# Seven block products for eight in one unit of each strip pair of the output product of an encoder block

## Chip, cores and metric

The kernel runs on one core of a Trainium2 chip. The metric is the time of one execution on the device in microseconds. The median of three timed runs of the kernel before is 1622.01 us (1621.78 to 1622.18).

## What is computed

One layer of an encoder over 256 tokens of width 2048, in float32: a combined input projection, a Mamba-2 branch in both directions, an attention branch, their gated sum, an output product with a residual, an MLP of width 8192, and a last norm. The change lies in the output product and its residual:

```
merged = sigmoid(gate_a) * branch_a + sigmoid(gate_b) * branch_b
x = x + merged @ w_out[layer]                 # (256 x 2048) @ (2048 x 2048)
h2 = rms_norm(x, g_mlp[layer])
x = x + jnp.square(jax.nn.relu(h2 @ w_mlp_in[layer])) @ w_mlp_out[layer]
return rms_norm(x, g_final)
```

## The kernel before

**Precision.** Every float32 operand of a product is split in two parts. ScalarE writes the high part (L637, `whi`), VectorE subtracts it from the raw piece for the low part (L1022, `wlo`), and TensorE makes three passes: high by high, high by low, low by high (`three_passes`, L1719 to L1721).

**Windows and pieces.** The work is a list of windows written out by hand in `walk`; every engine walks the same list. A window is a product of the 256 tokens with one strip of 512 columns of a weight matrix, in eight pieces of two row tiles each (512 KB, one load). For a piece TensorE issues 2 row tiles x 2 token blocks x 3 passes = 12 matmuls 512 columns wide. The output product is four windows, `out` 0 to 3; behind them stands the first window of the MLP.

**Positions.** Each engine runs, at each piece position, the splits that are due there and then the side work of the window, given as a list of names: `merged` (gates the product of the window before, adds the branches, turns the result and splits it), `residual` (adds a strip of the output product to `x_sb`, turns it by eight transposes, splits it and squares it). An engine's program order is fixed: what stands behind a waiting instruction waits too. PSUM is eight banks of 512 columns, the four of `G` and the four of `S`.

**Rings.** Up to the MLP the split weights have a ring of four slots: the copy on ScalarE of piece m waits until TensorE is done with piece m-4, and VectorE subtracts piece m at position m-2 of its own list. From the MLP on (`N_MLP`), the ring has eight slots (`whi_late`, `wlo_late`), and `count_due` lets both engines go up to seven blocks ahead. The raw pieces have four slots before the MLP and seven in it; SyncE issues the load of a piece once the low part of the piece that held its slot is made.

**Merged and output product.** The last window of the attention up-projection, (16, 1), fills `G[0:2]`. At position 0 of window (17, 0) VectorE makes the splits due there and then `gated`, which drains `G[0:2]` and raises `taken[1]`, and `merge_v`; TensorE turns the result behind piece 1. `out` 0 writes `G[2:4]` in all its eight pieces, `out` 1 writes `G[0:2]`. The last load of `x`, by SyncE, stands ahead of the load of piece 8 of the output product and waits for `merge_v` 4.

**Seven for eight.** In the MLP's second product the kernel already works with pairs of strips. A unit there is four row tiles by two strips, cut in 2 x 2 blocks of the tokens and of the weights. In a crossed unit VectorE makes four sums of weight blocks in place in the four raw slots (`difference`, L1025), four sums of the activations' blocks, and TensorE makes seven block products of 6 matmuls (`seven`) in place of four pieces of 12. Their results land in four banks, are copied out by ScalarE (L967) and added into `x_sb` in five additions by VectorE (L1515 to L1530).

Of the kernel before, what the change touches and what calls it, by code (L numbers as in the profile page):

```python
# [66 lines left out]
def walk(eng, window):  # L67
# [49 lines left out]
TURNED = 2  # L117
N_MLP = U_MLP * PIECES
# [11 lines left out]
MIX_OUT = {0: 4, 1: 5}  # L130
PAIR_PARTS = ((0, 0), (0, 1), (1, 1), (1, 0))
# [14 lines left out]

def crossed(n):

    at = pair_place(n)
    return at is not None and at[2] in CROSSED[at[1]]  # L150


def crossed_before(g, q, unit):

    return g * (len(CROSSED[0]) + len(CROSSED[1])) + q * len(CROSSED[0]) + CROSSED[q].index(unit)
# [6 lines left out]
def count_blocks():  # L162

    begin, at = [], 0
    for n in range(N_END):
        begin.append(at)
        if not crossed(n):
            at += 1
        elif pair_place(n)[3] == 3:
            at += len(PAIR_BLOCKS)  # L170
    return begin + [at]
# [5 lines left out]
def block_slot(m):  # L177
    return m % RING if m < N_MLP else (m - N_MLP) % LATE_RING

# [6 lines left out]
def released(n):  # L186

    if not crossed(n):
        return BLOCK[n] + 1
    part = pair_place(n)[3]  # L190
    return BLOCK[n] + (4, 5, 6, 7)[part]
# [12 lines left out]
def block_sources():  # L204

    out = []
    for n in range(N_END):
        if not crossed(n):
            out.append((n, None))
        elif pair_place(n)[3] == 3:  # L210
            out += [(n - 3, i) for i in range(len(PAIR_BLOCKS))]
    return out
# [20 lines left out]
def slot_free(m):  # L233

    if m < N_MLP + RING:
        return max(m - RING + 1, 0)
    return max(m - LATE_RING + 1, N_MLP)
# [24 lines left out]
def build(nc, x, x_t, w_in, w_dt, gains_in, taps_in, rows_in, w_ssm_up, w_attn_up, w_out, w_mlp_in, w_mlp_out,  # L262
# [208 lines left out]
    h_taken, c_taken = sem("h_taken"), sem("c_taken")  # L471
    mix_a, mix_v, x_mixed = sem("mix_a"), sem("mix_v"), sem("x_mixed")
# [46 lines left out]
    def out_product(j, tb):  # L519

        return S[:, 2 + tb, :] if j == 3 else product(j % 2, tb)
# [29 lines left out]
    def _(sp):  # L551
# [19 lines left out]
        def window(r, par, kind, idx, sides):  # L571
            for p in range(PIECES):
# [10 lines left out]
                if kind == "out" and (idx, p) in ((0, 0), (1, 0)):  # L583

                    sp.wait_ge(merge_v, 3 + idx)
                    for c in range(3 * idx, 3 + idx):
                        sp.dma_start(x_sb[:, c, :, :], x_k[:, :, c * N:(c + 1) * N]).then_inc(s_x[c], 16)
# [12 lines left out]
                elif kind == "mlp_pair":  # L600
                    g, q, unit, part = pair_place(n)
                    kh, half = PAIR_PARTS[part]
                    src = mats["mlp_out"][:, ds(g * KT + 4 * unit + 2 * kh, 2), (2 * q + half) * N:(2 * q + half + 1) * N]
                elif kind == "mlp_out":
# [27 lines left out]
    def _(act):  # L632
# [6 lines left out]
        def split(m):  # L639
# [5 lines left out]
            g, q, unit, _ = pair_place(n)  # L645
            turn = 4 * crossed_before(g, q, unit)
# [9 lines left out]
        def split_high(rnd, dst, k0, gain=None, factor=1.0):  # L656

            act.wait_ge(ts_t, rnd + 1)
# [5 lines left out]
            else:  # L664
                for c in range(4):
                    last = act.activation(dst[:, k0 + c, :], S[:, c // 2, c % 2 * T:(c % 2 + 1) * T],
# [250 lines left out]
        def residual(p, j, pr, pp):  # L917
            if p == 2:
                split_high(TS_X2 + j, a_hi, 4 * j, gain=1)
# [3 lines left out]
            if p == 7 and j == 3:  # L923
# [21 lines left out]

        def wide(t, h):
            return t[:, 2 * h:2 * h + 2, :].rearrange("p b n -> p (b n)")
# [25 lines left out]
        def finish(p, j, pr, pp):  # L973
            if p == (6 if j == 2 else 1 + j):
                act.wait_ge(c_taken, 14 + 2 * j)
                for tb in range(TB):
# [3 lines left out]
                                         residual, hidden, finish)}  # L980
        between_splits = {f.__name__: f for f in (carry_out, mix_out)}
# [37 lines left out]
    def _(dve):  # L1019
# [7 lines left out]
        def split(m):  # L1027
# [4 lines left out]
            g, q, unit, _ = pair_place(n)  # L1032
            turn = 4 * crossed_before(g, q, unit)
# [20 lines left out]
        def split_low(rnd, hi, lo, k0, gain=None, factor=1.0):  # L1054

            dve.wait_ge(ts_hi, rnd + 1)
# [6 lines left out]
            else:  # L1063
                for c in range(4):
                    k = gain * KT + k0 + c
                    last = dve.scalar_tensor_tensor(
                        out=lo[:, k0 + c, :], in0=S[:, c // 2, c % 2 * T:(c % 2 + 1) * T],
# [378 lines left out]
        def add_product(j, pr, pp, bank):  # L1446
            dve.wait_ge(used, done(pr, pp))
            dve.wait_ge(s_x[j], 16)
            for tb in range(TB):
                part = x_sb[:, j, tb, :]  # L1450
                last = dve.tensor_tensor(part, part, bank(tb), ALU.add)
            last.then_inc(taken[pp], 1)

        def residual(p, j, pr, pp):
            if p == 0:
                add_product(j, pr, pp, lambda tb: out_product(j, tb))
            if p == 2:
                split_low(TS_X2 + j, a_hi, a_lo, 4 * j, gain=1)
            if p == 4 and j == 3:
# [5 lines left out]
        def hidden(p, idx, pr, pp):  # L1465
# [15 lines left out]
            if p == 3 and j in SUMMED:  # L1481
                a11, a12 = hidden_u[:, 0:2, 0:P], hidden_u[:, 2:4, 0:P]
                a21, a22 = hidden_u[:, 0:2, P:T], hidden_u[:, 2:4, P:T]
                turn = 4 * (len(SUMMED) * g + j)
                dve.tensor_tensor(s_sum[:, 0, :, :], a21, a22, ALU.add).then_inc(s_v, 1)
                dve.tensor_tensor(s_sum[:, 2, :, :], a11, a21, ALU.subtract).then_inc(s_v, 1)
                dve.wait_ge(s_v, turn + 1)
                dve.tensor_tensor(s_sum[:, 1, :, :], s_sum[:, 0, :, :], a11, ALU.subtract).then_inc(s_v, 1)
                dve.wait_ge(s_v, turn + 3)
                dve.tensor_tensor(s_sum[:, 3, :, :], a12, s_sum[:, 1, :, :], ALU.subtract).then_inc(s_v, 1)  # L1490
# [65 lines left out]
        def finish(p, j, pr, pp):  # L1556
# [10 lines left out]
            if p == late + 2:  # L1567
                dve.wait_ge(c_taken, 14 + 2 * j)
                dve.wait_ge(s_g_last, 16)
                for tb in range(TB):  # L1570
# [3 lines left out]
                                         residual, hidden, sums, mixed, mix_out, finish)}  # L1574

        def window(r, par, kind, idx, sides):
            for p in range(PIECES):
                for m in due(piece_number(r, par, p), LEAD_LO):
                    split(m)
# [37 lines left out]
    def _(pool):  # L1617
# [73 lines left out]
        def residual(p, j, pr, pp):  # L1691
            if p == 4 and j == 3:
# [3 lines left out]
        table = {f.__name__: f for f in (rates, scan, zgate, rope, attend, residual)}  # L1696
# [16 lines left out]
    def _(pe):  # L1713
        operand = {"ssm_up": (b_hi, b_lo), "out": (b_hi, b_lo), "mlp_out": (b_hi, b_lo)}
# [21 lines left out]
        def transpose_round(src):  # L1736

            for c in range(4):
                for tb in range(TB):
                    last = pe.transpose(S[:, c // 2, c % 2 * T + tb * P:c % 2 * T + (tb + 1) * P],  # L1740
# [177 lines left out]
        def residual(p, j, pr, pp):  # L1918
            if p == 1:
                pe.wait_ge(taken[pp], pr + 1)  # L1920
                split_round(TS_X2 + j, lambda c, tb: x_sb[:, j, tb, c * P:(c + 1) * P])
            if p == 6 and j == 3:

                pe.wait_ge(rstd_x, 2)
# [5 lines left out]
        table = {f.__name__: f for f in (rates, decays, conv, scan, zgate, rope, attend, merged, residual)}  # L1930
# [13 lines left out]
        def seven(block, q, unit, m, start, stop):  # L1944
# [4 lines left out]
                    "b21": sums_bank(q, 0, 0), "b22": sums_bank(q, 1, 0), "t4": sums_bank(q, 0, 1)}  # L1949
            if block in ("b11", "t2", "t3", "t1"):  # L1950
                first_one, last_one = start, stop
            else:
                first_one, last_one = False, (block, q, unit) == ("b22", 1, 2)
# [3 lines left out]
            else:  # L1957
                i, tb = ("t1", "t2", "t3", "b22").index(block), 0
                hi, lo = s_hi[unit][:, i, :, :], s_lo[unit][:, i, :, :]
# [43 lines left out]

        def turned_window(r, idx, sides):
# [28 lines left out]
        def window(r, par, kind, idx, sides):  # L2033
            hi, lo = operand.get(kind, (a_hi, a_lo))
            if kind == "mlp_pair":
                pair_window(r, par, idx)
                return
            if kind == "xbc" and idx >= TURNED:
# [4 lines left out]
            elif kind == "mlp_in" and idx[0]:  # L2043
                if idx[1]:
                    pe.wait_ge(c_taken, 4 * idx[0])
                else:
                    pe.wait_ge(m_out, 4 * idx[0] - 1)
            elif kind == "mlp_out":
# [9 lines left out]
            rounds = {"ssm_up": TS_MERGED, "out": TS_X2, "mlp_in": TS_END}.get(kind)  # L2058
            ready = ts_lo
            late = (kind == "out" and idx == 0) or (kind == "mlp_in" and first(idx[0]) and idx[1] == 0)  # L2060
            into = product
            if kind == "out":
                into = lambda _, tb: out_product(idx, tb)
# [5 lines left out]
            for p in range(PIECES):  # L2069
                if (r, par) == (0, 0):  # L2070
                    pe.wait_ge(x_lo, 2 * p + 2)
                if p == 0 and rounds is not None:
                    pe.wait_ge(ready, rounds - 1 if late else rounds)
                if p == 0 and kind == "mlp_in" and idx[1] == 1:
                    pe.wait_ge(hid_hi, 1)
                if p == PIECES - 2 and late:
                    pe.wait_ge(ready, rounds)
# [95 lines left out]
```

## Time and profile before

| | |
|---|---|
| median of three runs | 1622.01 us |
| profiled execution, own time | 1622.15 us |
| its span, first to last instruction | 1620.0 us |
| output product, four windows (838.72 to 929.35 us of the span) | 90.63 us |
| TensorE (PE) busy in them | 90.63 us |
| VectorE (DVE) busy in them | 50.86 us |
| ScalarE (ACT) busy in them | 42.60 us |

The profile is of one execution. Times inside it run from the start of the span. Busy times of PE are of pipelined matmuls, which overlap each other; on VectorE and ScalarE too the end of one instruction overlaps the start of the next by a little.

### The profile page before, as it was taken

Reading aid. Unit: us, or ns where it says so; the run is one execution under the profiler, and the core shown is the slowest. Engines: PE = TensorE matmul, PEld = TensorE weight load, DVE = VectorE, ACT = ScalarE, POOL = GpSimd, SP = SyncE. Lnnn points to the kernel's source line nnn. Section 1 sums busy time; section 2 is a strip of 40 time slices with the busy share of each in tenths; the row PEclk is TensorE's granted clock in tenths of the full one; section 3 lists DMA queues with packets and bytes.
Section 4 is the critical chain, followed back from the end, with each engine's and each line's share of the span. In section 5 each row is a group of like instructions: output and inputs, shape, how many; then the busy total and the mean of one; then the engine's idle time right before and its main releaser. Section 6 shows DMA issues by size and latency. Waiting matters only on the chain.

```text
span 1620.0 us, 20751 instructions
## 1 busy us (share of the span) xinstructions
PE 1608.5 (99%) x8104; PEld 1362.2 (84%) x8104; DVE 1264.1 (78%) x1520; ACT 917.1 (57%) x1262; POOL 79.1 (5%) x67
## 2 busy tenths in 40 slices
PE   9999999999999999999999999999999999999998
PEld 7888888888888888888888888888888888888886
DVE  7888878888666677776665576999799988998893
ACT  6666556666565445544444555665556556655562
POOL 3000000000001134000000000000000000000000
PEclk9999999999999999999999999999999999999999
DMA  7666665666556664445576676458646764586471
GB/s 272 202 200 190 189 200 189 208 195 203 183 186 182 191 187 153 142 145 175 187 229 195 225 236 187 144 182 285 184 125 224 262 190 134 194 282 209 148 245 53
DMA packets 134194, 312.21 MB, mean 193 GB/s; under 512 B 9744, under 2 KB 10448, under 8 KB 133968
## 3 DMA queue, kind: packets, MB, share of 16 engines
q1 hardware_dynamic: 129376, 302.21, 58.4%
q10 hardware_dynamic: 4720, 8.68, 2.0%
q8 instruction: 64, 1.05, 0.3%
q14 instruction: 34, 0.28, 0.0%
HBM read 308.68 MB, written 2.16 MB: 192 GB/s over the span
## 4 chain that ended last, share of the span: by engine, by line
PE 96%; DVE 2%; issue 1%; ACT 0%; POOL 0%; DMA 0%; POOLq 0%; DVEq 0%
PE G L1719 17%; PE G L1720 17%; PE G L1721 17%; PE G L1728 13%; PE S L1728 7%; PE G L1732 6%; PE S L1719 4%; PE S L1721 4%; PE S L1720 4%; PE S L1732 4%; PE S L1740 1%; PE S L1847 1%; DVE wlo L1022 1%; PE S L1891 0%; PE S L1824 0%
## 5 line engine op out<-in xcount | busy, mean ns | idle before, releaser
L637 ACT ACTIVATE whi<-raw 128x1024 fp32r<-128x1024 f32 x395 | 417.0, 1059 | 418.1 <-PE G L1721 254.9
L1022 DVE TENSOR_TENSOR wlo<-raw,whi 128x1024 fp32r<-128x1024 f32 x395 | 482.5, 1236 | 128.7 <-ACT whi L637 127.4
L1719 PE MATMUL G<-whi,a_both 128*128 128x512 f32 x768 | 301.3, 392 | 2.3 <-DVE wlo L1022 1.7
L1721 PE MATMUL G<-whi,a_both 128*128 128x512 f32 x768 | 299.5, 390 | 0.0
L1720 PE MATMUL G<-wlo,a_both 128*128 128x512 f32 x768 | 299.5, 390 | 0.0
L1728 PE MATMUL G<-a_both,whi 128*128 128x512 f32 x640 | 201.7, 397 | 0.0
L1719 PEld LDWEIGHTS G<-whi,a_both 128*128 128x128 f32 x768 | 144.3, 188 | 33.3 <-issue 2.6
L1721 PEld LDWEIGHTS G<-whi,a_both 128*128 128x128 f32 x768 | 144.2, 188 | 30.1
L1720 PEld LDWEIGHTS G<-wlo,a_both 128*128 128x128 f32 x768 | 144.3, 188 | 28.7
L1732 PEld LDWEIGHTS G<-a_both,wlo 128*128 128x128 f32 x640 | 120.3, 188 | 28.2
L1719 PE MATMUL G<-whi,b_hi 128*128 128x512 f32 x342 | 133.9, 392 | 0.0
L1720 PE MATMUL G<-wlo,b_hi 128*128 128x512 f32 x342 | 133.6, 391 | 0.0
L1721 PE MATMUL G<-whi,b_lo 128*128 128x512 f32 x342 | 133.3, 390 | 0.0
L637 ACT ACTIVATE whi_late<-raw 128x1024 fp32r<-128x1024 f32 x85 | 88.9, 1058 | 67.2 <-PE S L1732 22.0
L1732 PE MATMUL G<-a_both,wlo 128*128 128x256 f32 x640 | 125.9, 278 | 0.0
L1022 DVE TENSOR_TENSOR wlo_late<-raw,whi_late 128x1024 fp32r<-128x1024 f32 x85 | 102.6, 1221 | 24.7 <-ACT whi_late L637 24.1
L637 ACT ACTIVATE whi_late<-gates 128x1024 fp32r<-128x1024 f32 x67 | 70.0, 1056 | 49.7 <-PE G L1732 17.9
L1728 PEld LDWEIGHTS G<-a_both,whi 128*128 128x128 f32 x640 | 97.6, 189 | 0.1
L1022 DVE TENSOR_TENSOR wlo_late<-gates,whi_late 128x1024 fp32r<-128x1024 f32 x67 | 81.1, 1221 | 18.7 <-ACT whi_late L637 18.6
L637 ACT ACTIVATE whi<-gates 128x1024 fp32r<-128x1024 f32 x63 | 66.2, 1056 | 38.2 <-PE G L1732 13.9
L1022 DVE TENSOR_TENSOR wlo<-gates,whi 128x1024 fp32r<-128x1024 f32 x63 | 76.3, 1222 | 12.5 <-ACT whi L637 12.0
L1728 PE MATMUL G<-a_both,whi_late 128*128 128x512 f32 x256 | 80.5, 396 | 0.0
(306 smaller groups left out, 2692.4 us busy)
## 6 DMA issues: line engine op xcount, KB each, us to landing
raw<-in_w_in SPq DMA_DIRECT2D x208, 512.0 KB, 4.3
raw<-in_w_mlp_in SPq DMA_DIRECT2D x74, 512.0 KB, 4.0
raw<-in_w_mlp_out SPq DMA_DIRECT2D x74, 512.0 KB, 5.0
gates<-in_w_mlp_in SPq DMA_DIRECT2D x54, 512.0 KB, 4.0
gates<-in_w_mlp_out SPq DMA_DIRECT2D x54, 512.0 KB, 4.9
raw<-in_w_ssm_up SPq DMA_DIRECT2D x32, 512.0 KB, 3.8
raw<-in_w_attn_up SPq DMA_DIRECT2D x32, 512.0 KB, 4.6
raw<-in_w_out SPq DMA_DIRECT2D x32, 512.0 KB, 4.6
```

The costliest lines, as they stand in the source:

```text
L637: act.activation(high(m), piece(n), ACT.Copy).then_inc(hi_made, 1)
L1022: dve.tensor_tensor(low(m), piece(n), high(m).bitcast(F32), ALU.subtract).then_inc(lo_made, 1)
L1719: pe.matmul(out_ap, hi[:, k, cols], w_hi, start=start, stop=False)
L1720: pe.matmul(out_ap, hi[:, k, cols], w_lo, start=False, stop=False)
L1721: return pe.matmul(out_ap, lo[:, k, cols], w_hi, start=False, stop=stop)
L1728: pe.matmul(banks[:, c, :], high(m)[:, cols[kk]], a_both[:, 2 * p + kk, :, :].rearrange("p h t -> p (h t)"), start=(p + kk == 0), stop=False)
L1732: last = pe.matmul(banks[:, c, 0:T], low(m)[:, cols[kk]], a_hi[:, 2 * p + kk, :], start=False, stop=(2 * p + kk == KT - 1))
L1740: last = pe.transpose(S[:, c // 2, c % 2 * T + tb * P:c % 2 * T + (tb + 1) * P], src(c, tb), ident[:, :])
L1847: last = pe.matmul(S[:, 2, (4 * c + h) * HD:(4 * c + h + 1) * HD], mw[:, 0, h, c, :], tm[:, c, h * HD:(h + 1) * HD], start=True, stop=True)
```

## The change

The four windows of the output product become two pairs of strips: window (17, 0) and (17, 1) are pair 0, (18, 0) and (18, 1) pair 1. Sixteen pieces of a pair go by units of four row tiles, each unit with the order (rows 0, strip 0), (rows 0, strip 1), (rows 1, strip 1), (rows 1, strip 0). Unit 2 (pieces 8 to 11 of the pair) is made of seven block products. The direct products of pair 0 go to `G` and its mixes to `S`; pair 1 the other way round. The ring of eight split slots and its schedule start with the output product (`N_OUT`), while the raw ring keeps its four slots up to the MLP.

```
-    window(16, 1, "attn_up", 3, [("merged", 2)])
-    window(17, 0, "out", 0, [("merged", 3)])
-    window(17, 1, "out", 1, [("residual", 0)])
-    window(18, 0, "out", 2, [("residual", 1)])
-    window(18, 1, "out", 3, [("residual", 2)])
-    window(19, 0, "mlp_in", (0, 0), [("residual", 3)])
+    window(16, 1, "attn_up", 3, [("merged", 2), ("blend", 0)])
+    window(17, 0, "out_pair", (0, 0), [("merged", 3)])
+    window(17, 1, "out_pair", (0, 1), [("out_mix", 0)])
+    window(18, 0, "out_pair", (1, 0), [("out_sums", 0)])
+    window(18, 1, "out_pair", (1, 1), [("out_mix", 1)])
+    window(19, 0, "mlp_in", (0, 0), [("out_sums", 1)])
...
+OUT_CROSSED = 2
+OUT_MIX = 4
...
-    return m % RING if m < N_MLP else (m - N_MLP) % LATE_RING
+    return m % RING if m < N_OUT else (m - N_OUT) % LATE_RING
...
-        if m < N_MLP + LEAD_HI:
+        if m < N_OUT + LEAD_HI:
             when.append(m - lead)
         else:
-            when.append(max(STEP[m - MLP_LEAD], STEP[m] - LEAD_HI - (m - N_MLP) // RING, N_MLP))
+            when.append(max(STEP[m - MLP_LEAD], STEP[m] - LEAD_HI - (m - N_OUT) // RING, N_OUT))
```

VectorE's new side work: `blend` makes the four sums of the activations of unit 2, `out_mix` adds the copied banks in two additions of 512 columns (position 5), two of 1024 (position 6) and one of 1024 (position 7), `out_sums` adds the direct products and splits the turned strips. `out_sums` stands ahead of the splits of its position.

```
+        def blend(p, _, pr, pp):
+            if p == 4:
...
+                dve.tensor_tensor(hidden_u, b_hi[:, k, :].bitcast(F32), b_lo[:, k, :].bitcast(F32), ALU.add
+                                  ).then_inc(o_v, 1)
+                dve.wait_ge(o_v, 1)
+                blocks_summed(o_v, 1)
+            if p == 5:
+                dve.wait_ge(o_hi, 1)
+                dve.tensor_tensor(s_lo[OUT_SET][:, :, :, :], s_sum, s_hi[OUT_SET][:, :, :, :].bitcast(F32), ALU.subtract
+                                  ).then_inc(o_lo, 1)
...
+        def out_mix(p, q, pr, pp):
+            m, own = m_acc[q], x_sb[:, 2 * q:2 * q + 2, :, :]
+            if p == OUT_MIX + 1:
...
+            if p == OUT_MIX + 2:
...
+            if p == OUT_MIX + 3:
...
+        def out_sums(p, q, pr, pp):
+            if p < 2:
+                j = 2 * q + p
+                dve.wait_ge(used, done(pr, pp))
+                dve.wait_ge(o_mixed, q + 1)
+                for tb in range(TB):
+                    part = x_sb[:, j, tb, :]
+                    dve.tensor_tensor(part, part, out_bank(q, p, tb), ALU.add).then_inc(o_taken, 1)
+            if p in (2, 3):
+                j = 2 * q + p - 2
+                split_low(TS_X2 + j, a_hi, a_lo, 4 * j, gain=1, banks=out_turned(q, p - 2))
```

ScalarE copies the four mix banks in two instructions at position 4 of the windows (17, 1) and (18, 1), ahead of the splits due there. TensorE:

```
+        def out_sums(p, q, pr, pp):
+            if p in (1, 2):
+                j = 2 * q + p - 1
+                pe.wait_ge(o_taken, 2 * j + 2)
+                transpose_round(lambda c, tb: x_sb[:, j, tb, c * P:(c + 1) * P], out_turned(q, p - 1)
+                                ).then_inc(ts_t, 1)
...
+        def out_window(r, par, idx, sides):
+            for p in range(PIECES):
+                n = piece_number(r, par, p)
+                q, unit, part = out_place(n)
+                if (unit, part) == (0, 0):
+                    if q:
+                        pe.wait_ge(o_mix, 2)
+                    else:
+                        pe.wait_ge(taken[0], r)
+                        pe.wait_ge(ts_lo, TS_X2 - 1)
+                if (q, unit, part) == (0, 0, 1):
+                    pe.wait_ge(taken[1], r)
+                if (unit, part) == (OUT_CROSSED, 0):
+                    pe.wait_ge(o_lo, 1)
+                    pe.wait_ge(ts_lo, TS_X2 + 2 * q)
...
```

## Rows read from the trace of the kernel before

**Rows 1.** The page: span, busy time of the engines.

```profile
span 1620.0 us, 20751 instructions
...
PE 1608.5 (99%) x8104; PEld 1362.2 (84%) x8104; DVE 1264.1 (78%) x1520; ACT 917.1 (57%) x1262; POOL 79.1 (5%) x67
```

**Rows 2.** TensorE's waits for other engines, two longest of four: us, times, longest.

```profile
PE G L1719 <- DVE wlo L1022: 1.7, 2, 1.3
PE S L1752 <- DVE tmp_a L1074: 1.5, 1, 1.5
```

**Rows 3.** Busy time by stretch: the output product's four windows.

```profile
core 0: us, PE busy (x) PEld busy (x) DVE busy (x) ACT busy (x) POOL busy (x), PEclk, DMA share, GB/s
838.72:929.35 90.63, 90.63 (x417) 75.41 (x417) 50.86 (x55) 42.60 (x58) 0.00 (x0) 1.00 0.64 205
```

**Rows 4.** Groups by shape, 832 to 950 us: splits and strip additions.

```profile
L1022 DVE TENSOR_TENSOR wlo<-raw,whi 128x1024 fp32r<-128x1024 f32 x39 | 47.4, 1223 | 33.3 <-ACT whi L637 33.3
L637 ACT ACTIVATE whi<-raw 128x1024 fp32r<-128x1024 f32 x39 | 41.2, 1061 | 54.6 <-PE G L1721 40.8 <-PE S L1721 11.6 <-DMA raw<-in_w_out 2.3
L1719 PE MATMUL G<-whi,b_hi 128*128 128x512 f32 x96 | 37.7, 392 | 0.0
```

**Rows 5.** Timeline of TensorE, start of `out` 0: its 1st and 13th matmul, the transposes.

```profile
838.56 0.39 PE L1719 MATMUL G<-whi,b_hi 128*128 128x512 f32 x1
...
841.28 0.39 PE L1719 MATMUL G<-whi,b_hi 128*128 128x512 f32 x1
...
844.00 1.03 PE L1740 MATMUL S<-ident,tmp_b 128*128 128x128 f32 x8
```

**Rows 6.** Timeline of VectorE at the start of `out` 0.

```profile
838.76 1.28 DVE L1423 SCALAR_TENSOR_TENSOR gates<-gates,G 128x512 f32<-128x512 f32 x2 [0.34 <-PE G L1721]
840.08 1.23 DVE L1441 TENSOR_TENSOR tmp_b<-gates 128x1024 f32<-128x1024 f32 x1
```

**Rows 7.** ScalarE and VectorE at 929 us, where the eight-slot ring starts now.

```profile
929.43 1.06 ACT L637 ACTIVATE whi<-raw 128x1024 fp32r<-128x1024 f32 x1 [1.66 <-PE S L1721]
...
930.52 1.23 DVE L1022 TENSOR_TENSOR wlo<-raw,whi 128x1024 fp32r<-128x1024 f32 x1 [1.49 <-ACT whi L637]
931.66 1.22 DVE L1022 TENSOR_TENSOR wlo_late<-gates,whi_late 128x1024 fp32r<-128x1024 f32 x1
932.80 1.28 DVE L1451 TENSOR_TENSOR gates<-gates,S 128x512 f32<-128x512 f32 x2
```

**Rows 8.** VectorE in the MLP: a crossed unit's pace, then a pair's mixes.

```profile
1083.76 1.22 DVE L1022 TENSOR_TENSOR wlo<-gates,whi 128x1024 fp32r<-128x1024 f32 x1
1084.90 1.22 DVE L1025 TENSOR_TENSOR gates<-gates 128x1024 f32<-128x1024 f32 x1
...
1114.00 0.69 DVE L1515 TENSOR_TENSOR mt<-mt 128x512 f32<-128x512 f32 x1
...
1115.34 1.22 DVE L1022 TENSOR_TENSOR wlo<-gates,whi 128x1024 fp32r<-128x1024 f32 x1
...
1119.13 1.22 DVE L1524 TENSOR_TENSOR gates<-gates,mt 128x1024 f32<-128x1024 f32 x1
1120.38 1.23 DVE L1526 TENSOR_TENSOR mt<-mt 128x1024 f32<-128x1024 f32 x1
```

**Rows 9.** ScalarE in the MLP: the copies of four mix banks.

```profile
1052.46 1.92 ACT L967 ACTIVATE mt<-S 128x1024 f32<-128x1024 f32 x2
```

**Rows 10.** Loads: landing of 28 from 833.6 us, then 8 in a burst (1043 to 1051).

```profile
L610 SPq DMA_DIRECT2D raw<-in_w_out x28: 367/368/368, 833.6 to 909.2; - x28
...
DMA to landing us min/median/max: 3.8/4.5/5.9
...
DMA to landing us min/median/max: 4.3/6.8/7.3
```

**Rows 11.** Stretches at the ends of the span: TensorE's gaps, and its clock.

```profile
20.00:25.00 5.00, 3.69 (x17) 2.76 (x16) 3.34 (x2) 5.00 (x7) 4.84 (x3) 1.00 0.91 322
...
1610.00:1620.00 10.00, 2.40 (x11) 1.67 (x9) 2.69 (x7) 2.03 (x6) 0.94 (x1) 0.79 0.28 106
```

More of the change, by code:

```diff
@@ L582, in window @@
                     rope_parameters()
-                if kind == "out" and (idx, p) in ((0, 0), (1, 0)):
-                    sp.wait_ge(merge_v, 3 + idx)
-                    for c in range(3 * idx, 3 + idx):
+                if kind == "out_pair" and (idx[0], p) == (0, 0):
+                    half = idx[1]
+                    sp.wait_ge(merge_v, 3 + half)
+                    for c in range(3 * half, 3 + half):
                         sp.dma_start(x_sb[:, c, :, :], x_k[:, :, c * N:(c + 1) * N]).then_inc(s_x[c], 16)
@@ L654, in split, with split_high @@
             high_part(m, n)
-        def split_high(rnd, dst, k0, gain=None, factor=1.0):
+        def split_high(rnd, dst, k0, gain=None, factor=1.0, banks=(S, 0)):
+            bank, b0 = banks
             act.wait_ge(ts_t, rnd + 1)
@@ L1052, in split, with split_low @@
                 low_part(m, n + i - 3)
-        def split_low(rnd, hi, lo, k0, gain=None, factor=1.0):
+        def split_low(rnd, hi, lo, k0, gain=None, factor=1.0, banks=(S, 0)):
+            bank, b0 = banks
             dve.wait_ge(ts_hi, rnd + 1)
@@ L1444, in merged, with blocks_summed @@
                 split_low(j + TS_MERGED, b_hi, b_lo, j * 4, factor=0.5)
[L1446 to L1459, printed above, removed]
+        def blocks_summed(signal, before):
+            a11, a12 = hidden_u[:, 0:2, 0:P], hidden_u[:, 2:4, 0:P]
+            a21, a22 = hidden_u[:, 0:2, P:T], hidden_u[:, 2:4, P:T]
+            dve.tensor_tensor(s_sum[:, 0, :, :], a21, a22, ALU.add).then_inc(signal, 1)
+            dve.tensor_tensor(s_sum[:, 2, :, :], a11, a21, ALU.subtract).then_inc(signal, 1)
+            dve.wait_ge(signal, before + 1)
+            dve.tensor_tensor(s_sum[:, 1, :, :], s_sum[:, 0, :, :], a11, ALU.subtract).then_inc(signal, 1)
+            dve.wait_ge(signal, before + 3)
+            dve.tensor_tensor(s_sum[:, 3, :, :], a12, s_sum[:, 1, :, :], ALU.subtract).then_inc(signal, 1)
@@ L1942, in last_window, with seven @@
                 last.then_inc(fin_mm, 1)
-        def seven(block, q, unit, m, start, stop):
+        def seven(block, q, unit, m, start, stop, sums=sums_bank, set_of=None):
             a11, a12 = (slice(4 * unit + 2 * i, 4 * unit + 2 * i + 2) for i in range(2))
@@ L1952, in seven @@
             else:
-                first_one, last_one = False, (block, q, unit) == ("b22", 1, 2)
+                first_one, last_one = False, set_of is None and (block, q, unit) == ("b22", 1, 2)
             if block in left:
@@ L2002, in pair_window @@
                     last.then_inc(used, 1)
+        def out_window(r, par, idx, sides):
+            for p in range(PIECES):
+                n = piece_number(r, par, p)
+                q, unit, part = out_place(n)
+                if (unit, part) == (0, 0):
[9 more added lines that the diff above has]
+                    pe.wait_ge(ts_lo, TS_X2 + 2 * q)
+                m = BLOCK[n]
+                if unit == OUT_CROSSED:
+                    for i in range(2 * part, min(2 * part + 2, len(PAIR_BLOCKS))):
+                        pe.wait_ge(lo_made, m + i + 1)
+                        seven(PAIR_BLOCKS[i], q, unit, m + i, True, True, out_bank, OUT_SET).then_inc(used, 1)
+                else:
+                    kh, half = PAIR_PARTS[part]
+                    pe.wait_ge(lo_made, m + 1)
+                    for kk in range(2):
+                        k, cols = 4 * unit + 2 * kh + kk, slice(kk * N, (kk + 1) * N)
+                        for tb in range(TB):
+                            last = three_passes(out_bank(q, half, tb), k, tb, b_hi, b_lo, high(m)[:, cols],
+                                                low(m)[:, cols], k == 0, k == KT - 1)
+                    last.then_inc(used, 1)
+                for name, at in sides:
+                    if name in table:
+                        table[name](p, at, *previous(r, par))
         def turned_window(r, idx, sides):
@@ L2056, in window @@
                 pe.wait_ge(taken[par], r)
-            rounds = {"ssm_up": TS_MERGED, "out": TS_X2, "mlp_in": TS_END}.get(kind)
+            rounds = {"ssm_up": TS_MERGED, "mlp_in": TS_END}.get(kind)
             ready = ts_lo
-            late = (kind == "out" and idx == 0) or (kind == "mlp_in" and first(idx[0]) and idx[1] == 0)
+            late = kind == "mlp_in" and first(idx[0]) and idx[1] == 0
             into = product
-            if kind == "out":
-                into = lambda _, tb: out_product(idx, tb)
             if kind == "mlp_out":
```

153 lines of the change are left out of this document (102 added, 51 removed).

## The prediction

> **What bounds the kernel now.** I read the page first: TensorE is busy for 1608.5 of 1620.0 us, VectorE for 1264.1 [rows 1]. Then its waits for other engines: the longest are 1.7 and 1.5 us in total, and they lie at the start of the kernel [rows 2]. Then the stretch that the change touches: in the four windows of the output product TensorE is busy for 90.63 of 90.63 us, VectorE for 50.86, ScalarE for 42.60 [rows 3]. So TensorE sets the time, a matmul that goes is worth its whole issue time, and every wait that the change gives TensorE is paid in full. VectorE's 40 us of idle time are cover, as long as its program order lets it be there in time.
>
> **What one matmul is worth.** The group of the output product's matmuls says 392 ns each [rows 4]. That is the time one of them is in the array, and the next starts before it ends. The timeline has the pace: the first matmul of `out` 0 starts at 838.56, the 13th at 841.28 and the transposes behind the 24th at 844.00 [rows 5], so 12 matmuls take 2.72 us, 0.227 us each. A sum with 392 ns would be off by a factor of 1.7.
>
> **What is removed.** A unit of four pieces has 48 matmuls. Made of seven block products it has 7 x 6 = 42. Two units are changed: 12 matmuls, 12 x 0.227 = 2.72 us. The transposes stay eight rounds in number. So 2.72 us (0.17% of 1622) is the most that this can give, whatever else goes well. A difference under 0.2%, 3.2 us, is about what a measurement of this kernel can't tell from none.
>
> **What is added, off TensorE.** By pace in a dense stretch an instruction of 1024 columns on VectorE takes 1.14 us [rows 8]. Over the whole stage: 6 more low parts and 8 weight sums, 14 x 1.14 = 16.0; two `out_mix` of 1.34 (two additions of 512 columns) + three of 1024 at 1.14 to 1.25, 5.0 us each [rows 8]; `blend` about 4 us. Together some 30 us on top of 50.86, over about 90: near 90% busy, against 56%. ScalarE gets 6 copies more and 4 double-bank copies of 0.96 us [rows 4, 9]; it stays under 60%. `blend` lies at positions 4 and 5 of the window before; a low part is made there over 5 us before TensorE wants it, so I cost it at nothing; without that cover it would be up to 4 us. The question is where these 30 us and the new order make TensorE late. I walked the three places at which it now waits for VectorE.
>
> **First deadline: the bank of strip 1.** Before, `out` 0 writes `G[2:4]` for a whole window, and `G[0:2]`, which the last attention window filled, has 21 us to be drained. Now the second piece of the pair writes `G[0:2]`, so TensorE waits at 841.28 for `taken[1]`. VectorE drained it from 838.76 to 840.04 before [rows 6], in time. But the eight-slot ring now starts here, and its schedule puts the splits of blocks 2, 3 and 4 at position 0, ahead of `gated`. Blocks 3 and 4 need copies that ScalarE can only start when TensorE is done with the window. This very pattern is in the trace at the MLP's first window, where the eight-slot ring starts before the change: ScalarE's copy starts at 929.43, VectorE's two low parts at 930.52 and 931.66, and only then, at 932.80, its next side work, 3.37 us behind the copy [rows 7]. There nobody wanted it early. Moved to the output product (the copy at 838.82), `gated` starts at 842.19 and ends 1.28 later, 843.47 [rows 6, 7]. TensorE resumes at about 843.5 in place of 841.28: **2.2 us lost**. The sum for `tmp_b` then ends at 844.7, before the transposes want it. If VectorE could drain first, nothing would be lost; if the raw piece of block 4 lands late, up to 1 us more (landings spread from 3.8 to 5.9 us [rows 10]).
>
> **Second deadline: the turned strips of pair 0.** TensorE wants to turn strip 0 behind the second piece of pair 1, that is 14 pieces and one unit of 42, 210 matmuls, and 0.8 us of transposes after 838.56: 887.0, with the first loss 889.2. It needs the two additions of `out_sums` at position 0, and these stand in VectorE's order behind all the splits that are due up to there, seven blocks ahead of TensorE, and behind the five additions of `out_mix`. Is VectorE seven blocks ahead? The crossed unit is what spoils it: its four sums are made in place, so it holds all four raw slots until its 4th, 5th, 6th and 7th low part are made. Its own loads are late too: the load of piece 8 stands behind the last load of `x`, which waits for `merge_v` 4, now at 844.7. Taking 5.3 us for it (behind another load, between median and longest [rows 10]), the unit's first low part starts at 852.2, and 11 instructions of 1.14 us with small gaps bring its last low part to 865.4. From there a slot's round is: load 4.5 (the median [rows 10]), copy 1.06, low part 1.23 [rows 4]. I get the low parts of the next unit at 866.2, 868.7, 869.8 and 871.0, the next three from 873.1 to 876.7. ScalarE puts its two mix copies (1.92 us [rows 9]) ahead of the next copy, whose low part starts at 879.5. From then on VectorE is dense: 4 low parts (4.56), `out_mix` (4.97), the two additions (1.28, as for `gates` [rows 7]) end at 890.3. TensorE wants them at 889.2: **1.1 us lost**. Bounds: nothing, if the loads take 3.8 us, and 5.3 us, if they take 5.9, because three rounds of loads lie in the chain (3 x 1.4 more).
>
> **Third deadline: the turned strips of pair 1**, behind the second piece of the MLP's first window. The same chain with better cover: the direct pieces of pair 1 load without the wait for `x`, and three of the MLP's raw slots are fresh. I get the additions done some 0.7 us before TensorE's wish: nothing lost, at most 2.
>
> Splits of the turned strips are wanted by the MLP's pieces 4 and 6 only; I find 3 us and more of room. From the MLP on, everything is as before, with the ring already full where it used to fill; since TensorE did not wait there, nothing is gained.
>
> **The sum.** -2.72 + 2.2 + 1.1 + 0 = +0.6 us. Against the profiled execution's own 1622.15 us this makes 1622.75; it was 0.14 above the median of 1622.01, so 1622.6, and with small semaphore gaps on a dense VectorE I say 1622.8.
>
> **The clock.** In the stretch from 20 to 25 us TensorE stood still for 1.3 us and the granted clock stayed 1.00, the 2.4 GHz level; it read 0.79 only at the end, where TensorE was busy for 2.4 of 10 us [rows 11]. The Trainium skill (TensorE: Matmul & The Clock Gate, section "HAM oscillation — how this bites in real kernels") says that gaps in TensorE's work can put it back to the low clock, so that what comes next starts cold; the trace shows no such fall for a gap of 1.3 us, and no gap of 2.2 us with work behind it. As a mechanism here: if the clock fell to 1.2 GHz after the first gap, two pieces at twice 2.72 us would cost 5.4 us, 1628. I give it 0.03.
>
> **Rivals.**
> 1. *The forecast*: a first wait of about 2.2 us, a second of 0 to 3, the gain given back. 1621.4 to 1624.5. Chance 0.62.
> 2. *VectorE's backlog decides* (slower): the same second deadline, but landings under the refill's load are nearer to those of a burst, median 6.8 [rows 10]. With 5.9 us the second wait is 5.3: 1622.0 - 2.72 + 2.2 + 5.3 = 1626.8. It decides from a mean landing of 5.4 us on, where the waits together pass 6 us. For it: nearly 90% busy VectorE, four raw slots. Against it: loads at this spacing took 4.5. Chance 0.16; from 1625.2 to 1629.
> 3. *No first wait*: `gated` comes in time, or TensorE's queue absorbs it, and VectorE keeps up: 1622.0 - 2.7 = 1619.3, to 1620.6. Against it: rows 7 show the order. Chance 0.15.
> 4. *The clock*: 0.03, 1628.
> 5. *A gain that I can't name*, under 1618.8: 0.04. The matmuls alone don't reach it.
>
> **How the numbers follow.** Likeliest: 1622.8, its own range 1621.4 to 1624.5. The range for 8 in 10 takes in nearly all of rival 3 below and the nearer half of rival 2 above: 1619.6 to 1626.4. Faster by over 0.2% (under 1618.8): 0.04. Slower (over 1625.3): 0.16 + 0.03, less the edge of rival 2, 0.17. Within: 0.79.
>
> **What the profile after would show.** The waits of TensorE: one of about 2.2 us at 841.3, at its 13th matmul on `G` in the output product, for VectorE's `gated`; one of about 1 us near 889 at the transposes of strip 0, for the additions of `out_sums`; none at the MLP's start. The output product and the MLP's first window together 0.6 us longer. VectorE some 80 us busy in the stage. I am wrong if `gated` runs before the splits of blocks 3 and 4, if VectorE is idle ahead of `out_sums` (then the second wait is not its backlog), or if the loads of the pieces behind a crossed unit take over 5.4 us.

## The result and the profile after

The changed kernel takes 1627.15 us (median of 7 runs, 1625.88 to 1631.62) against 1622.01 us before; the ratio is 1.0035, with a 95% interval of 1.0023 to 1.0047. It is slower by about 5 us, and its runs spread over 5.7 us where those of the kernel before spread over 0.9. That lies above the range of the prediction. The profiled execution took 1626.85 us with a span of 1624.7 us, 4.7 more than before.

The page of the kernel after, its span and the engines' busy times:

```profile
span 1624.7 us, 20781 instructions
...
PE 1608.4 (99%) x8092; PEld 1360.7 (84%) x8092; DVE 1293.1 (80%) x1550; ACT 928.4 (57%) x1273; POOL 79.1 (5%) x67
```

Beside [rows 1]: twelve matmuls fewer, yet TensorE is busy as long, and VectorE 29 us longer, the 30 that were counted. TensorE's waits after, us in total, times, longest (beside [rows 2]):

```profile
PE G L1827 <- DVE gates L1545: 2.6, 1, 2.6
PE G L1805 <- DVE gates L1472: 2.2, 1, 2.2
PE G L1805 <- DVE wlo L1071: 1.7, 2, 1.3
```

Two waits are new: for `gated` (L1472) and for the additions of `out_sums` (L1545). They lie at the 13th matmul of the output product and at the transposes of strip 0. TensorE's timeline after:

```profile
841.25 0.39 PE L1807 MATMUL G<-whi,b_lo 128*128 128x512 f32 x1
843.81 0.50 PE L1805 MATMUL G<-whi,b_hi 128*128 128x512 f32 x1 [2.17 <-DVE gates L1472]
...
845.51 0.63 PE L1805 MATMUL G<-whi,b_hi 128*128 128x512 f32 x1
845.94 0.63 PE L1806 MATMUL G<-wlo,b_hi 128*128 128x512 f32 x1
...
848.08 1.22 PE L1827 MATMUL S<-ident,tmp_b 128*128 128x128 f32 x8
...
891.09 0.39 PE L1807 MATMUL S<-whi_late,b_lo 128*128 128x512 f32 x1
894.10 1.09 PE L1827 MATMUL G<-ident,gates 128*128 128x128 f32 x8 [2.62 <-DVE gates L1545]
```

Behind the first wait something else is new: from 845.1 us on a matmul starts every 0.43 us instead of every 0.227, down to the transposes. The busy times by stretch have the reason in the column PEclk, the granted clock:

```profile
843.80:844.80 1.00, 0.99 (x4) 0.86 (x5) 1.00 (x1) 0.80 (x2) 0.00 (x0) 1.00 0.84 291
844.80:845.80 1.00, 1.00 (x4) 0.80 (x3) 1.00 (x2) 0.99 (x1) 0.00 (x0) 0.62 0.38 148
845.80:846.80 1.00, 1.00 (x4) 0.71 (x4) 1.00 (x2) 0.00 (x0) 0.00 (x0) 0.50 0.29 84
846.80:847.80 1.00, 1.00 (x4) 0.80 (x3) 0.48 (x1) 0.00 (x0) 0.00 (x0) 0.50 0.97 311
847.80:848.80 1.00, 1.00 (x7) 0.80 (x6) 0.00 (x0) 0.00 (x0) 0.00 (x0) 0.68 0.99 262
```

The clock fell to 0.50, the 1.2 GHz level, 1.2 us after TensorE had resumed at 843.81, and was back at 1.00 before 848.8. From the restart to the first matmul behind the transposes TensorE took 5.24 us (843.81 to 849.05), against 3.51 before (841.28 to 844.79). Behind a gap at which the clock stayed at 1.00 (`gap2` below) the same stretch took 3.69. So the slow clock costs some 1.6 us, and the restart itself 0.2.

VectorE after, ahead of the two waits:

```profile
840.11 1.23 DVE L1071 TENSOR_TENSOR wlo<-raw,whi 128x1024 fp32r<-128x1024 f32 x1 [1.49 <-ACT whi L671]
841.34 1.23 DVE L1071 TENSOR_TENSOR wlo_late<-raw,whi_late 128x1024 fp32r<-128x1024 f32 x1
842.48 1.28 DVE L1472 SCALAR_TENSOR_TENSOR gates<-gates,G 128x512 f32<-128x512 f32 x2
...
877.48 1.22 DVE L1071 TENSOR_TENSOR wlo_late<-raw,whi_late 128x1024 fp32r<-128x1024 f32 x1 [1.16 <-ACT whi_late L671]
880.39 1.23 DVE L1071 TENSOR_TENSOR wlo_late<-raw,whi_late 128x1024 fp32r<-128x1024 f32 x1 [1.68 <-ACT whi_late L671]
883.16 2.36 DVE L1071 TENSOR_TENSOR wlo_late<-raw,whi_late 128x1024 fp32r<-128x1024 f32 x2 [1.55 <-ACT whi_late L671]
885.44 0.68 DVE L1523 TENSOR_TENSOR mt<-mt 128x512 f32<-128x512 f32 x1
...
892.75 1.28 DVE L1545 TENSOR_TENSOR gates<-gates,G 128x512 f32<-128x512 f32 x2
```

`gated` stands behind two low parts, as the pattern of [rows 7] said, where it started at 838.76 in [rows 6]. From 877 to 883 us VectorE stands still by turns, for ScalarE's copies; then it is dense up to the additions. ScalarE's own waits, and the landings (the time from the issue of a load until its data are there) of all 32 loads of the output product, say what the copies wait for:

```profile
ACT whi L671 <- DMA raw<-in_w_out: 15.0, 12, 2.7
ACT whi_late L671 <- DMA raw<-in_w_out: 8.3, 8, 2.2
```

```profile
L644 SPq DMA_DIRECT2D raw<-in_w_out x32: 367/368/701, 822.7 to 912.2; - x32
...
DMA to landing us min/median/max: 3.7/5.7/9.2
```

[rows 10] has 28 of the 32 loads before. All 32 of them landed in 3.8 to 8.8 us, the median 4.6, and ScalarE waited for one of them only, 2.3 us. So the middle moved by about 1 us, and the long ones are not new. On ScalarE, the copies that VectorE's dense stretch hangs on:

```profile
871.46 1.06 ACT L671 ACTIVATE whi<-raw 128x1024 fp32r<-128x1024 f32 x1 [0.94 <-DMA raw<-in_w_out]
...
879.29 1.06 ACT L671 ACTIVATE whi_late<-raw 128x1024 fp32r<-128x1024 f32 x1 [1.84 <-DMA raw<-in_w_out]
880.26 1.92 ACT L963 ACTIVATE mt<-S 128x1024 f32<-128x1024 f32 x2
882.07 2.01 ACT L671 ACTIVATE whi_late<-raw 128x1024 fp32r<-128x1024 f32 x2
```

Two loads lie in this chain. One was issued at 865.8, when the crossed unit set its slot free, and took 5.7 us; the next, into the slot that this piece had used, was issued at 873.8 and took 5.5. Then come the two mix copies and the copy behind them, and at 883.16 VectorE's low part.

### The profile page after: what moved, and what is told of

It is laid out like the page before. It is cut to its first block, busy times and chain, and to the rows that moved or that the text cites. A ratio compares the mean times of both kernels' runs of the same rounds, so it can differ in the third digit from the quotient of the medians.

```text
span 1624.7 us, 20781 instructions
## 1 busy us (share of the span) xinstructions
PE 1608.4 (99%) x8092; PEld 1360.7 (84%) x8092; DVE 1293.1 (80%) x1550; ACT 928.4 (57%) x1273; POOL 79.1 (5%) x67
## 4 chain that ended last, share of the span: by engine, by line
PE 92%; DVE 4%; DMA 2%; issue 1%; ACT 1%; POOL 0%; POOLq 0%; DVEq 0%; ACTq 0%
PE G L1805 16%; PE G L1806 15%; PE G L1807 15%; PE G L1814 13%; PE S L1814 7%; PE G L1818 6%; PE S L1805 4%; PE S L1807 4%; PE S L1806 4%; PE S L1818 4%; DMA raw<-in_w_out 1%; DVE wlo L1071 1%; PE S L1934 1%; PE S L1827 1%; DMA raw<-in_w_in 0%
## 5 line engine op out<-in xcount | busy, mean ns | idle before, releaser
L671 ACT ACTIVATE whi<-raw 128x1024 fp32r<-128x1024 f32 x377 | 397.7, 1059 | 386.5 <-PE G L1807 209.8
L1071 DVE TENSOR_TENSOR wlo<-raw,whi 128x1024 fp32r<-128x1024 f32 x377 | 460.8, 1238 | 105.4 <-ACT whi L671 104.7
L671 ACT ACTIVATE whi_late<-raw 128x1024 fp32r<-128x1024 f32 x109 | 114.4, 1058 | 82.5 <-PE G L1818 20.0
L1071 DVE TENSOR_TENSOR wlo_late<-raw,whi_late 128x1024 fp32r<-128x1024 f32 x109 | 131.9, 1221 | 30.9 <-ACT whi_late L671 29.7
L1805 PE MATMUL G<-whi,b_hi 128*128 128x512 f32 x248 | 97.6, 394 | 2.2 <-DVE gates L1472 2.2
L671 ACT ACTIVATE whi<-gates 128x1024 fp32r<-128x1024 f32 x67 | 70.2, 1058 | 49.5 <-PE G L1818 19.0
L1806 PE MATMUL G<-wlo,b_hi 128*128 128x512 f32 x248 | 97.4, 393 | 0.0
L1807 PE MATMUL G<-whi,b_lo 128*128 128x512 f32 x248 | 97.2, 392 | 0.0
L1071 DVE TENSOR_TENSOR wlo<-gates,whi 128x1024 fp32r<-128x1024 f32 x67 | 80.9, 1220 | 14.7 <-ACT whi L671 14.2
L1071 DVE TENSOR_TENSOR wlo_late<-gates,whi_late 128x1024 fp32r<-128x1024 f32 x63 | 76.3, 1220 | 17.5 <-ACT whi_late L671 17.1
```

The lines of the kernel that those rows point to most:

```text
L671: act.activation(high(m), piece(n), ACT.Copy).then_inc(hi_made, 1)
L1071: dve.tensor_tensor(low(m), piece(n), high(m).bitcast(F32), ALU.subtract).then_inc(lo_made, 1)
L1805: pe.matmul(out_ap, hi[:, k, cols], w_hi, start=start, stop=False)
L1806: pe.matmul(out_ap, hi[:, k, cols], w_lo, start=False, stop=False)
L1807: return pe.matmul(out_ap, lo[:, k, cols], w_hi, start=False, stop=stop)
```

## The experiments

The theory after the result (B): VectorE is late at the additions because the copies ahead of them wait for loads, and the loads for the four raw slots, which the crossed unit holds; what TensorE loses before that point is hidden in this wait. The rivals: the losses simply add up (A), or VectorE has too much work of its own. And apart from these: what does a gap in TensorE's work cost?

**VectorE drains first.** In VectorE's list of window (17, 0):

```
+                early = kind == "out_pair" and (idx, p) == ((0, 0), 0)
+                for m in blocks[:1] if early else blocks:
+                    split(m)
+                if early:
+                    merged(p, 3, *previous(r, par))
+                    for m in blocks[1:]:
+                        split(m)
+                    continue
```

> One edit to the changed kernel: VectorE does gated (and the sum for tmp_b) ahead of the splits of blocks 3 and 4 at position 0 of window (17, 0). Theory A (each loss of TensorE stands by itself: first wait 2.3, slow clock 1.8, second wait 2.8 us): the first wait and the slow stretch go, 1627.15 - 4.1 = about 1623. Theory B (the second wait is for VectorE's backlog behind late loads, so whatever TensorE wins before it is lost there again): first wait gone, wait at the transposes of strip 0 grows from 2.6 to about 6 us, total 1625.5 to 1627.5.

1627.55 us (1626.47 to 1628.66), ratio 1.0031 (1.0019 to 1.0043). As B said, with the time at the upper edge of what it allowed. TensorE's longest wait, a half microsecond inside it, and the stretches around it:

```profile
PE G L1834 <- DVE gates L1545: 6.1, 1, 6.1
```

```profile
892.50:893.00 0.50, 0.00 (x0) 0.00 (x0) 0.50 (x1) 0.00 (x0) 0.00 (x0) 0.50 0.71 209
```

```profile
891.00:894.00 3.00, 0.26 (x1) 0.26 (x2) 2.90 (x5) 0.84 (x1) 0.00 (x0) 0.69 0.52 164
894.00:897.00 3.00, 3.00 (x12) 2.71 (x12) 3.00 (x4) 1.25 (x4) 0.00 (x0) 0.50 0.36 115
897.00:900.00 3.00, 3.00 (x11) 2.30 (x11) 2.81 (x6) 2.48 (x6) 0.00 (x0) 0.68 0.26 94
```

The first wait is gone and so is the slow stretch behind it, and TensorE is at the transposes 3.9 us earlier (893.74 - 6.12 against 894.10 - 2.62). VectorE is not: its additions start at 892.40 instead of 892.75. So nearly all that was won is waited away. And the clock now falls here, where nothing hides it: it reads 0.50 from about 892.1 on, 1.6 us before TensorE resumes, until about 899. From the first round of transposes to the second TensorE takes 6.1 us, against 3.7 in the first profile of the changed kernel, where the clock stayed at 1.00.

**Seven raw slots.**

```
-    return n % RING if n < N_MLP else (n - N_MLP) % LATE_RAW
+    return n % RING if n < N_OUT else (n - N_OUT) % LATE_RAW
...
-                elif n >= N_MLP:
-                    sp.wait_ge(merge_v, 4)
+                elif n >= N_OUT:
+                    sp.wait_ge(merge_v, 3)
```

> One edit to the changed kernel: the raw pieces have seven slots from the output product on (the three slots of the gates buffer that the MLP uses), instead of four. Theory B: the loads behind the crossed unit no longer wait for it, VectorE has its lead back, the second wait goes (under 0.5 us); what is left is the first wait of 2.3 and the slow clock of 1.8 us, less 2.7: about 1623.4. Rival (VectorE's own work of 90% is the backlog, not the loads): second wait stays over 1.5 us, 1625 or more.

1623.28 us (1621.79 to 1623.79), ratio 1.0003 (0.9994 to 1.0012). The second wait is gone, as B said; the first (2.1 us) stays, and in the profiled run the slow clock behind it. The eleven runs stand in two groups, six at 1623.28 to 1623.79 with mean granted clocks of 0.997 and 0.998, five at 1621.79 to 1622.54 with 0.998 and 0.999: it looks as if the clock fell in the first group alone. Its additions start at 887.9 us, 4.9 earlier, although its loads take as long to land as in the changed kernel (medians 5.9 and 6.0 us for the two halves of the ring): three more slots hide them.

**Both.**

> Both edits. Theory B: no wait of TensorE in the output product, no slow clock, the 12 matmuls' 2.7 us are gained: 1619.3. Rival (VectorE's own work): a wait of 1 to 5 us at the transposes of strip 0 stays, 1620.5 to 1625.

1619.81 us (1619.35 to 1620.22), ratio 0.9984 (0.9975 to 0.9993). This version beats both kernels: 2.5 us under the 1622.31 of the kernel before on the same chip, of the 2.72 that the twelve matmuls are worth. The waits of TensorE that are left lie at the start of the kernel, and the clock reads 1.00 over the whole product. The two longest of these waits, and the stretch from the start of the output product on:

```profile
PE G L1812 <- DVE wlo L1071: 1.9, 2, 1.4
PE S L1846 <- DVE tmp_a L1123: 1.5, 1, 1.5
```

```profile
838.70:932.00 93.30, 93.30 (x435) 77.86 (x434) 81.96 (x84) 55.70 (x66) 0.00 (x0) 1.00 0.67 229
```

VectorE is busy for 81.96 of 93.30 us here, with all the change's work, and TensorE for all of them. So VectorE's own work was not the bound.

**A gap and nothing else.** In the kernel before TensorE is made to wait for `taken[1]`, and VectorE does 2, 3 or 4 additions that nobody needs ahead of raising it (`gap2`, `gap3`, `gap4`; the lines are those of `gap3`):

```
+            if slot == 7:
+                for dst in (mt[:, 0, :, :], mt[:, 1, :, :], m_acc1[:, 0:2, :], m_acc1[:, 2:4, :])[:3]:
+                    dve.tensor_tensor(dst, gates[:, 3, :, :], gates[:, 3, :, :], ALU.add)
...
+                if kind == "out" and (idx, p) == (0, 1):
+                    pe.wait_ge(taken[1], r)
```

> The kernel before with one gap in TensorE's work and nothing else: TensorE waits for taken[1] ahead of the second piece of out 0, and VectorE does three additions of 1024 columns (into memory not used here) ahead of gated. The gap is 840.04 + 3 x 1.14 - 841.28 = 2.2 us. If a gap costs its own length: 1624.2. If the granted clock falls behind it, as for 3.4 us in the changed kernel: 1.6 to 1.8 us more, 1626.

> As gap3, with two additions ahead of gated: a gap of about 1.1 us in TensorE's work in place of 2.2. Without a fall of the clock 1622.3 + 1.1 = 1623.4; with a fall as long as in gap3, about 1625. The stretch from 20 to 25 us in the kernel before had 1.3 us of gaps at a clock of 1.00, so I expect 1623.4.

> As gap3, with four additions ahead of gated: a gap of about 3.3 us in TensorE's work. With its length alone 1625.6; with a fall of the clock in every run, which I expect as it fell behind 2.1 us, 1.7 us more, 1627.3.

| wait in the profile | time | over the kernel before, run beside it | ratio, 95% | granted clock behind it |
|---|---|---|---|---|
| 0.9 us | 1623.88 | +1.33 | 1.0009 (1.0000 to 1.0018) | stayed 1.00 |
| 2.1 us | 1625.14 | +2.83 | 1.0018 (1.0009 to 1.0027) | fell (profiled run) |
| 3.2 us | 1627.47 | +5.17 | 1.0033 (1.0020 to 1.0045) | fell |

The stretches behind the gap of 2.1 us, then three of 1 us behind that of 3.2:

```profile
842.80:846.80 4.00, 3.49 (x8) 2.77 (x9) 3.95 (x4) 0.00 (x0) 0.00 (x0) 0.58 0.01 3
846.80:850.80 4.00, 4.00 (x23) 3.40 (x22) 0.72 (x2) 2.03 (x3) 0.00 (x0) 1.00 0.92 306
```

```profile
845.00:846.00 1.00, 1.00 (x3) 0.80 (x3) 1.00 (x2) 0.00 (x0) 0.00 (x0) 0.50 0.00 0
846.00:847.00 1.00, 1.00 (x4) 0.74 (x3) 1.00 (x1) 0.00 (x0) 0.00 (x0) 0.50 0.00 0
847.00:848.00 1.00, 1.00 (x4) 0.81 (x3) 1.00 (x2) 0.00 (x0) 0.00 (x0) 0.50 0.00 0
```

A gap of 3.2 us costs 2.0 us more than its length. One of 2.1 us costs 0.7 more in the median, and 1.4 in the profiled run, where the clock fell (1625.85 us against a median of 1622.31 before). That the clock falls in part of the runs only is borne out by the mean granted clock of each run: the five from 1625.85 to 1626.35 us have 0.997, the six from 1624.30 to 1625.14 have 0.998 or 0.999, as the kernel before. Where in the kernel it fell is shown for the profiled run alone. For the gap of 0.9 us the excess, 0.4, is not clear of the noise.

**The strips turned two pieces later.** In `out_sums` of ScalarE, VectorE and TensorE, for pair 0:

```
-            if p in (1, 2):
-                j = 2 * q + p - 1
+            later = 0 if q else 2
+            if p - later in (1, 2):
+                n = p - later - 1
+                j = 2 * q + n
```

> One edit to the changed kernel: the strips of pair 0 are turned two pieces later (behind pieces 4 and 5 of pair 1 in place of 2 and 3), their splits with them. If the second wait is VectorE's lateness at one deadline, two pieces (5.4 us) of room hide its 2.8 us and it does not come back: 1627.15 - 2.8 = 1624.3, with the first wait and the slow clock as they were. If VectorE simply has too much work in this stage, the wait turns up again at a later reader (the crossed unit of pair 1, or the MLP's start) and the time stays near 1627.

1628.36 us (1627.55 to 1629.35), ratio 1.0037 (1.0024 to 1.0049). My expectation missed; the second half of its text is what happened. The wait at pair 0 went and stood again at the MLP's first window, 939.4 us, for the additions of pair 1, with the clock falling behind it:

```profile
PE S L1829 <- DVE gates L1546: 2.8, 1, 2.8
PE G L1807 <- DVE gates L1473: 2.1, 1, 2.1
```

More room at one reader does not give VectorE back its time: in the changed kernel the second wait was also what let it catch up for the third place. It did so barely: there the additions of pair 1 ended at 938.4 us and the transposes started at 938.46.

**The last load of `x` later.**

```
-                if kind == "out_pair" and (idx[0], p) == (0, 0):
+                if kind == "out_pair" and (idx, p) in (((0, 0), 0), ((0, 1), 4)):
```

> One edit to the changed kernel: SyncE issues the last load of x four pieces later (ahead of piece 12 of pair 0, not of piece 8). If that load, which waits for merge_v 4 and takes its share of the transfer, is what makes the crossed unit's pieces late, they land some 1 to 2 us earlier, the second wait shrinks from 2.6 to about 1.5 and the time is about 1626. If the four raw slots alone make the backlog, nothing changes: 1627.

1626.16 us (1624.16 to 1628.85), ratio 1.0023 (1.0014 to 1.0032). The additions start at 890.7 instead of 892.8 us, so this load has a part in the lateness. In the time it is 3.6 us over the kernel before beside it, where the changed kernel was 5.1 and 5.9 over on other chips: some 1.5 to 2.3 us less, with a spread of 4.7 us between its own runs. In its profiled run the clock did not fall behind the first wait of 2.1 us, but behind the second of 2.3.

**The ring alone.** The kernel before with `N_OUT` for `N_MLP` in `block_slot`, `count_due` and `slot_free`:

> One part of the change alone: the kernel before, with its four plain windows of the output product, and the eight-slot ring and its schedule from the output product on. Nobody wants G[0:2] early here, so no first wait; the sum for tmp_b is late for the transposes at 844.0 by about 0.7 us. No crossed unit holds the raw slots, so VectorE gets its seven blocks of lead: no wait, or up to 1.5 us, at the first residual. Expected 1622.3 to 1624. If the schedule alone were the loss (VectorE's additions behind seven blocks of splits), 1625 or more.

1623.40 us (1622.79 to 1624.30), ratio 1.0005 (0.9996 to 1.0014) against 1622.55: a wait of 0.6 us at the transposes of `tmp_b`, and no other behind the start of the kernel. So the schedule seven blocks ahead is not by itself the loss.

**The crossed unit made plain.** `crossed` gives False for the output product, and TensorE's window follows it. The side work stays, but the weight sums and the seven products are left out; `out_mix` then adds banks that hold nothing of this unit, so the output is not the encoder's:

```
     if out_place(n) is not None:
-        return out_place(n)[1] == OUT_CROSSED
+        return False
```

> The changed kernel with unit 2 of each pair in four plain pieces of 12 matmuls instead of seven block products; the pairs, the ring, the order, blend, out_mix and out_sums are kept, so that out_mix adds four banks that hold no product of this unit: the output is not the reference's. If it is the crossed unit's hold on the four raw slots (with its weight sums) that makes VectorE late, the second wait goes: 1622.2 + first wait 2.3 + slow clock 1.8 = 1626.3, or 1624.5 where the clock does not fall. If the order alone (additions behind splits for seven blocks and out_mix) does it, the second wait stays at 2 us or more: 1628.

1625.08 us (1624.41 to 1626.83), ratio 1.0019 (1.0010 to 1.0028). With twelve matmuls more it is faster than the changed kernel. Its waits:

```profile
PE G L1805 <- DVE gates L1472: 2.3, 1, 2.3
PE G L1805 <- DVE wlo L1071: 1.8, 2, 1.4
```

The second is gone. The crossed unit, with its hold on four slots and its weight sums, is what makes VectorE late; of these two it is the hold that costs, since with seven slots the same sums did no harm.

**The changed kernel again.**

> The changed kernel again, unedited, for a second profile beside these: two waits of about 2.2 and 2.6 us; the granted clock falls behind one of them or both. 1626 to 1628.

1628.19 us (1627.47 to 1630.22), ratio 1.0038 (1.0023 to 1.0054). Waits of 2.1 and 2.9 us. This time the clock fell behind both; the stretches behind the second:

```profile
894.00:897.00 3.00, 2.67 (x13) 2.29 (x14) 3.00 (x5) 1.54 (x5) 0.00 (x0) 0.73 0.36 106
897.00:900.00 3.00, 3.00 (x13) 2.41 (x12) 3.00 (x6) 2.19 (x6) 0.00 (x0) 0.70 0.48 154
```

The profiled run took 1628.46 us, 1.6 more than the one in which the clock fell behind the first wait only. The totals alone do not show the cause, as a wait at the start of the kernel was 0.5 us longer too (0.8 against 0.3). The stretch does: from the first round of transposes to the second it is 5.28 us (894.33 to 899.61) against 3.71 (894.10 to 897.81), 1.6 us for this fall.

## Why the prediction was wrong

- **The matmuls' worth** (2.72 us) was right: 2.5 us came out once nothing was in their way, and with an interval that leaves out 1 (0.9975 to 0.9993), although it is under the 0.2% that the prediction took for the limit of what can be told.
- **The first deadline** was right in place, cause and size: 2.2 us predicted, 2.17 seen, at the 13th matmul. Alone (with seven raw slots) it and what follows it leave 1623.28, the gain given back.
- **The second deadline is the step that failed.** Its place and mechanism were as described; the term mis-sized was the landing of the loads at and behind the crossed unit, taken as the median of the kernel before, 4.5 us [rows 10] (5.3 for piece 8). Those loads stood some 2.7 us apart. Close together the two in the chain took 5.7 and 5.5 us, and the first three of the unit, behind the load of `x`, 6.5, 7.1 and 7.9. The additions ended at 894.0 us, not 890.3. Of these 3.7 us the crossed unit's own loads brought 1.5 (its last low part ended at 866.9, not 865.4) and the two refill loads 2.2. So the three rounds of loads lie in the chain as the prediction's bound had them, each longer than its 4.5. That was rival 2, with its threshold of 5.4 us; its count for landings of 5.9, the transposes 5.3 us behind 889.2, comes to 894.5 against the 894.1 seen. Its chance of 0.16 was too low, given that the burst of [rows 10] was in hand.
- **The third deadline** was met in the changed kernel, as predicted, but only because TensorE had stood still at the second: with the strips of pair 0 turned later it cost 2.8 us.
- **The clock** was given 0.03 and 5.4 us. The chance was too low and the price too high: every profile with a wait of 2.1 us or more has a fall at one of its waits or both, for 3.4 us each, worth 1.6 us of TensorE's time; at the wait of 6.1 us it was 6.8 us, worth 2.4. The longest gap in the trace before with work on both sides of it was 1.3 us [rows 11], and there was no evidence for longer ones. The Trainium skill (TensorE: Matmul & The Clock Gate, section "HAM oscillation — how this bites in real kernels") said that gaps put TensorE back to the low clock. These traces agree in part: 0.50 behind waits of 2.2, 3.2 and 6.1 us and 1.00 behind 0.9, but also 1.00 behind waits of 2.1 (`x` late) and 2.6 us (changed kernel, second wait).
- **The sum, rebuilt.** Up to the transposes of strip 0 the count is VectorE's: without any loss TensorE would have been there at 887.0, it started them at 894.1. That is 7.1 us less the 2.7 that the two units save, 4.4, and 0.2 of it is a later start of the output product. The slow clock behind the first wait lies inside the 7.1 and adds nothing; the second wait would be that much longer without it, as VectorE's drain first shows. Behind the second wait it adds 1.6 us in the runs where it falls, and that is the likely source of the spread; two profiles bear it out, and the slowest of the seven runs (1631.62 us) has a mean granted clock of 0.996 where the others have 0.997. Of the remaining 0.3 us of the span's 4.7, 0.2 is the restart behind the second wait (3.71 us for 12 matmuls and a round of transposes, 3.51 before).

Open is what decides in which runs the clock falls: in stretches it is known of the profiled runs only. Open is also whether the additions of `out_sums`, put ahead of the splits and of `out_mix` on VectorE, would have been in time with four slots; that was not run.

## What to carry to other kernels

Where an edit hands a bank or a schedule to a stage earlier than before, list what each engine now does ahead of the first reader in its program order: here one drain behind two splits cost as much as the whole gain. Moving one call had it back, but only once the second wait was gone (seven slots, 1623.28 to 1619.81 us); with four slots the same move brought nothing. A unit that works in place in a ring of loads holds the ring; size the ring so that the refill, at the landing times of close loads, is hidden, and do not take these times from a stretch where the loads stood apart. Here a wait of TensorE of 2.1 to 3.2 us cost its length and, where the clock fell, 1.6 us on top, 0.2 us for the restart besides.

## What the runs showed of the hardware that was not expected

When the granted clock fell to 0.50 it did not fall at one fixed place against TensorE's work. Behind waits of 2.1 to 3.2 us it fell after TensorE had resumed: 0.1 us after in `gap3`, 0.2 in `gap4`, 1.2 behind the first wait of the changed kernel. At the wait of 6.1 us (VectorE drains first) it fell 4.5 us into the wait, 1.6 us before TensorE resumed. In the kernel before TensorE's last matmul ended at 1612.4 us, and the clock read 0.50 only from 1616 on.

By rows of half a microsecond it stayed at 0.50 for 3.4 us in every one of the ten falls behind waits of 2.1 to 3.2 us, and for 6.8 us at the wait of 6.1. It did not fall behind 0.9 us, and behind a wait of 2.1 to 2.6 us it fell in some executions and not in others of nearly the same code (the second wait of the changed kernel: not in the first profile, in the second with 2.9 us; the first wait with `x` late: not).

The landing of 512 KB took 3.7 us at least and 9.2 at most for the loads of one stage (3.8 to 8.8 before). In the refill of the changed kernel it followed the spacing: the load at 862.2 us, 9 us behind the one before it, took 3.7; the next four, issued 1.1 to 2.4 us apart, took 4.8, 5.7, 5.8 and 5.7.
